# Sample states of branch A: four 32-row tiles on half-width spreads, one set of four banks

## What is computed

```python
def step(S, inp):
    r_t, w_t, k_t, v_t, kk_t, b_t = inp
    sk = jnp.einsum('bhvk,bhk->bhv', S, kk_t)
    S = S * w_t[:, :, None, :] - sk[..., None] * b_t[:, :, None, :] + v_t[..., None] * k_t[:, :, None, :]
    return S, jnp.einsum('bhvk,bhk->bhv', S, r_t)
S, ys = lax.scan(step, s_wkv.astype(f32), xs)
```

## Time and profile before

| what | value |
|---|---|
| median of three runs | 1308.31 us |
| lowest and highest run | 1305.56 us, 1309.54 us |
| the profiled execution's own time | 1308.13 us |
| its span, first to last instruction | 1306.4 us |
| PE busy | 1243.1 us (95%) |
| DVE busy | 862.6 us (66%) |
| ACT busy | 551.2 us (42%) |
| granted TensorE clock, mean | 0.984 |

### The profile page before, as it was taken

How to read it: one execution, slowest core, us unless ns; L and a number is a source line. 1 busy time by engine, 2 the same in 40 slices (tenths; PEclk the granted TensorE clock), 3 DMA queues, 4 the chain that set the end, 5 groups by cost and what they waited for, 6 DMA issues and landing times.

```text
span 1306.4 us, 27689 instructions
## 1 busy us (share of the span) xinstructions
PE 1243.1 (95%) x11984; PEld 1167.4 (89%) x11984; DVE 862.6 (66%) x1440; ACT 551.2 (42%) x841; POOL 128.4 (10%) x144
## 2 busy tenths in 40 slices
PE   6999999999998999999899998999999989999996
PEld 5899887898997999999798987888899979999996
DVE  4887568877766665653477954688777657566433
ACT  5553434443445433343444533344444454333432
POOL 0004473000000000000000071900000000000000
PEclk9999999999998999999999999999999989999998
DMA  6433235544353644544433323355444534444441
GB/s 225 129 116 115 66 104 177 196 146 146 127 168 101 189 146 149 157 146 147 144 97 113 125 75 86 95 181 181 145 147 134 160 101 145 147 154 146 151 149 69
DMA packets 51176, 179.50 MB, mean 137 GB/s; under 512 B 6256, under 2 KB 7024, under 8 KB 49776
## 3 DMA queue, kind: packets, MB, share of 16 engines
q1 hardware_dynamic: 42576, 153.77, 37.7%
q10 hardware_dynamic: 8480, 23.97, 5.2%
HBM read 166.57 MB, written 8.53 MB: 134 GB/s over the span
## 4 chain that ended last, share of the span: by engine, by line
PE 81%; DVE 8%; ACT 3%; POOL 3%; DMA 2%; issue 2%; ACTq 0%; SPq 0%; DVEq 0%; POOLq 0%
PE dense L1310 50%; PE core L1310 31%; DVE w_lo L857 2%; ACT w_hi L564 1%; DMA wkv_s<-s_st 1%; DVE x L905 1%; POOL qk_rot L521 1%; DVE y_out L903 1%; POOL rot_tmp L519 1%; POOL qk_rot L518 1%; DMA qk_rot<-qk_raw 1%; DMA x<-x_t 0%; POOL s_st L532 0%; DVE bonus L968 0%; DVE y_a L1164 0%
## 5 line engine op out<-in xcount | busy, mean ns | idle before, releaser
L857 DVE TENSOR_TENSOR w_lo<-w_raw,w_hi 128x1024 fp32r<-128x1024 f32 x282 | 350.9, 1245 | 237.3 <-ACT w_hi L564 236.8
L564 ACT ACTIVATE w_hi<-w_raw 128x1024 fp32r<-128x1024 f32 x282 | 298.0, 1057 | 474.8 <-PE dense L1310 317.3
L1310 PE MATMUL dense<-h_hi,w_hi 128*128 128x320 f32 x1296 | 418.4, 323 | 28.7 <-DVE h_lo L861 14.6
L1310 PE MATMUL dense<-h_hi,w_lo 128*128 128x320 f32 x1296 | 404.9, 312 | 0.0
L1310 PE MATMUL dense<-h_lo,w_hi 128*128 128x320 f32 x1296 | 404.8, 312 | 0.0
L1310 PEld LDWEIGHTS dense<-h_hi,w_hi 128*128 128x128 f32 x1296 | 247.0, 191 | 45.0 <-issue 33.5
L1310 PEld LDWEIGHTS dense<-h_lo,w_hi 128*128 128x128 f32 x1296 | 247.6, 191 | 4.3 <-issue 2.4
L1310 PEld LDWEIGHTS dense<-h_hi,w_lo 128*128 128x128 f32 x1296 | 247.3, 191 | 0.0
L1310 PE MATMUL core<-h_hi,w_hi 128*128 128x320 f32 x416 | 129.5, 311 | 0.0
L1310 PE MATMUL core<-h_lo,w_hi 128*128 128x320 f32 x416 | 129.0, 310 | 0.0
L1310 PE MATMUL core<-h_hi,w_lo 128*128 128x320 f32 x416 | 129.0, 310 | 0.0
(11 more groups left out here) (295 smaller groups left out, 1987.9 us busy)
## 6 DMA issues: line engine op xcount, KB each, us to landing
w_raw<-wts SPq DMA_DIRECT2D x282, 512.0 KB, 3.5
ret_t<-ret_t ACTq DMA_DIRECT2D x16, 256.0 KB, 3.7
ret_s<-ret_t ACTq DMA_DIRECT2D x16, 256.0 KB, 2.4
ret_rest<-ret_d ACTq DMA_DIRECT2D x2, 1536.0 KB, 6.6
qk_rot<-qk_raw SPq DMA_DIRECT2D x8, 320.0 KB, 6.2
dmask<-rconst ACTq DMA_DIRECT2D x2, 1152.0 KB, 5.6
s_st<-wkv_st ACTq DMA_DIRECT2D x2, 1024.0 KB, 5.0
wkv_s<-s_st ACTq DMA_DIRECT2D x2, 1024.0 KB, 8.1
```

The lines of the kernel that those rows point to most:

```text
L564: act.activation(w_hi[n % RING][:, :], w_raw[n % RING][:, :], ACT.Copy).then_inc(hi_ready.sem, 1)
L857: dve.tensor_tensor(w_lo[r][:, :], w_raw[r][:, :], w_hi[r][:, :].bitcast(F32), ALU.subtract).then_inc(low_made.sem, 1)
L1310: return pe.matmul(out, lhsT, rhs, start=start, stop=stop)
```

## The change

The spreads have 4 blocks instead of 8 (256 columns instead of 512): block s holds the tokens of sequence s of the first four and, in the other 32 rows of the half, those of sequence s + 4, since the pattern `F_SEQ` now repeats after four. So the rows 32q to 32q + 31 of a half (q = 0, 1) give the states of the sequences 4q to 4q + 3. A pair is eight matmuls of 32 rows by 64 output rows by 256 columns: the two heads, the two values of q, and v and u. All v results of q lie in `of_v[q]`, all u results in `of_u[q]`; these are four banks, half filled, and the same four for every pair. So a pair waits for the adds of the pair right before it, and the first pair for the add of the sample outputs (`y`), which lie in `core[3]`. DVE adds in four steps of 256 columns, three of them waited for. The spreads lie in other places (L200), which takes the wait for the transposed values out of the first one (L1051). `TAIL` has another order, and the first tile that opens `dense[2]` again waits for `s3` instead of `s2`.

```diff
-TAIL = [("gate", 0), ("s", 0), ("mean", 0), ("mean", 1), ("s", 1), ("gate", 1), ("mean", 2), ("mean", 3), ("s", 2), ("s", 3),
-        ("var", 0), ("var", 1), ("gate", 2), ("var", 2), ("var", 3)]
+TAIL = [("gate", 0), ("s", 0), ("mean", 0), ("mean", 1), ("s", 1), ("gate", 1), ("s", 2), ("mean", 2), ("mean", 3), ("gate", 2),
+        ("var", 0), ("var", 1), ("s", 3), ("var", 2), ("var", 3)]
...
-        v_exp, u_exp = [at("v_exp0", 20, 512), at("v_exp1", 22, 512)], [at("u_exp0", 32, 512), at("u_exp1", 34, 512)]
+        v_exp, u_exp = [at("v_exp0", 20, 256), at("v_exp1", 21, 256)], [at("u_exp0", 22, 256), at("u_exp1", 23, 256)]
...
-        def state_banks(h):
-
-            return (core[3], core[2]) if h % 2 else (dense[2], core[4])
+        of_u, of_v = (dense[2], core[3]), (core[4], core[2])
...
-                    return dve.tensor_tensor(to[h % 2][:, :].rearrange("p (s c) -> p s c", s=NSEQ), bc(of, 1, NSEQ),
-                                             bc(fx[:, F_SEQ:F_SEQ + NSEQ], 2, C), ALU.mult)
+                    return dve.tensor_tensor(to[h % 2][:, :].rearrange("p (s c) -> p s c", s=4), bc(of, 1, 4),
+                                             bc(fx[:, F_SEQ:F_SEQ + 4], 2, C), ALU.mult)
...
-                    if h == 0:
-                        dve.wait_ge(*v_turned(layer, 7))
...
-                        link(dve.tensor_tensor(st, st, state_banks(h)[0][:, :], ALU.add))
-                        dve.tensor_tensor(st, st, state_banks(h)[1][:, :], ALU.add).then_inc(seq_evac.sem, 1)
+                        for q in range(2):
+                            part = st[:, 256 * q:256 * q + 256]
+                            link(dve.tensor_tensor(part, part, of_v[q][:, 0:256], ALU.add))
+                            ins = dve.tensor_tensor(part, part, of_u[q][:, 0:256], ALU.add)
+                            if q == 0:
+                                link(ins)
+                        ins.then_inc(seq_evac.sem, 1)
...
-                        pe.wait_ge(*seq_evac(layer, EVAC_AT["s2", SAMPLE]))
+                        pe.wait_ge(*seq_evac(layer, EVAC_AT["s3", SAMPLE]))
...
-                        evac("ys", NCHUNK - 1)
-                    elif h == 1:
                         evac("y", SAMPLE)
                     else:
-                        evac(f"s{h - 2}", SAMPLE)
+                        evac(f"s{h - 1}", SAMPLE)
                     tk = step_mats(tok, SAMPLE, 128)[:, h, :]
-                    of_u, of_v = state_banks(h)
-                    across(of_v[:, :], tk[:, 0:C], v_exp[h % 2][:, :])
-                    done(halves(of_u[:, :], tk[:, C:2 * C], u_exp[h % 2][:, :]))
+                    for of, keys, spread, crossed in ((of_v, tk[:, 0:C], v_exp, 1), (of_u, tk[:, C:2 * C], u_exp, 0)):
+                        for q in range(2):
+                            for half in range(2):
+                                rows, to = slice(C * half + 32 * q, C * half + 32 * q + 32), C * (half ^ crossed)
+                                ins = mm(of[q][to:to + C, 0:256], keys[rows], spread[h % 2][rows, :])
+                    done(ins)
...
-    fixed[:, F_SEQ:F_SEQ + NSEQ] = (i // SEQ_S)[:, None] == np.arange(NSEQ)
+    fixed[:, F_SEQ:F_SEQ + NSEQ] = (i // SEQ_S % 4)[:, None] == np.arange(NSEQ)
```

More of the change, by code:

```diff
@@ L136 @@
 FILL = (2, 2, 1)
-ACT_STEPS, DVE_STEPS, POOL_STEPS = 13, 221, 18
+ACT_STEPS, DVE_STEPS, POOL_STEPS = 13, 229, 18
 def program(nc, x_t, wts, pvec, lora, shift0, fixed, rmask, trig, rconst, wkv_st, ret_d, ret_t,
```

## The result

The changed kernel takes 1300.82 us (median of nine runs, 1298.24 to 1303.85) against 1307.26 us before (nine runs, 1304.56 to 1309.57). The ratio is 0.9946, 95% interval 0.9930 to 0.9962: faster by 0.54%, 6 to 7 us (5.0 to 9.2 by the interval). The forecast was 1305.8 and its range began at 1303.6, so it was wrong: the gain is some three times as large. The profiled execution of the changed kernel is its fastest, 1298.24 us with a span of 1296.5.

What follows compares the result with a forecast made beforehand. PE was taken to set the pace inside the stage, with slack behind it, where time counts only through DVE's low part; 1308.1 + 0.3 (first layer) - 1.1 (second layer) - 1.5 (clock) = 1305.8 us, range 1303.6 to 1309.8.

Steps and rivals of the forecast that it cites:

- The products: PE's pair of matmuls in the stage: 0.62 us instead of 1.02, with eight 32-row tiles at work at once.
- two row tiles of one bank take turns: Rival at the pairs: four passes, 1.0 us a pair as now, total 1307.8 us; chance 0.08.
- The new wait: At pair 1 PE waits 1.7 us for DVE's adds of pair 0.
- the sum: Whole kernel: 1308.1 + 0.3 - 1.1 - 1.5 = 1305.8 us, the saving of all four pairs spent at pair 1.
- Pair 2: In the first layer PE waits 0.8 us for DVE's adds of pair 1, held behind a gain by ACT's lateness.
- "shorter wait" rival: Low part at 204.11 runs undisturbed, pair 1's wait 0.6 us shorter per layer: about 1304.5; 0.11 including luck with transfers.
- 0.55 us later: First head products behind the stage start 0.55 us late in each layer.
- The store and what follows: Second layer: store ahead of the weight load lands sooner than 9.28 us, so DVE's low part comes 1.1 us sooner.
- My 6.5: Landing time in us taken for the second layer's store of the states, between 5.0 and 9.3.
- my 2.3 for both layers: Forecast change over both layers: 0.3 us more in the first, 1.1 less in the second, 1.5 less for the clock.
- The clock at 898: Behind the second layer's second head products the fall at 898.6 stays away, saving 1.5 us.
- about 0.03 for four more starts: Term in the 0.62 us pair: about 0.03 us for PE's four added matmul starts.

Runs made afterwards that it cites:

- `pad64`: The kernel before with 16 inert fp32 matmuls (64 TensorE records) added ahead of the first pair of layer 1: 1302.31 us, ratio 0.9962.
- `before_again`: The kernel before, unchanged, measured once more: 1307.97 us, ratio 0.9993.
- `tiles_only`: The changed kernel with the old order of `TAIL` put back, keeping 32-row tiles and one set of four banks: 1312.62 us, ratio 1.0050 against the kernel before.
- `tail_only`: The kernel before with the new order of `TAIL` alone, 64-row tiles and two sets of banks kept: 1305.07 us, ratio 0.9987.
- `after_pad68`: The changed kernel with 17 more 8-column matmuls in layer 1, giving it 48 whole instruction blocks: 1301.85 us, ratio 0.9945 against the kernel before.
- `after_low1`: The changed kernel with DVE's four low parts in the rounds one round earlier in both layers: 1307.45 us, ratio 0.9993 against the kernel before.

## Why the prediction was wrong, step by step

- **The products**: right, 0.62 us. The rival that two row tiles of one bank take turns (1.0 us) is refuted here: `core` and `dense` banks each took two row tiles, on different halves of their rows, and all eight records of a pass started within 0.05 us, with the pair at 0.62 us. By the packing rate of the Trainium skill ("TensorE: Matmul & The Clock Gate", section "Part 3: Packing small matmuls — row/col tiling"), 3.07 for four 32-row tiles, the pair would have been an estimated 0.75 us; the trace has 0.62 us and shows no such loss. "No row of before has 32-row tiles" was not quite so: the trace has 16 records of 32 by 128 (`lora_w`, in layer 1 from 55.3 us on), but they start 0.37 us or more apart and say nothing of tiles at work together.
- **The new wait** at pair 1: 1.58 and 1.10 us for 1.7, right in size. It eats the gain of the tiles, as the sum said.
- **Pair 2**: wrong. I took ACT's lateness there for something "the change does not touch". In that execution ACT waited for POOL's rotations, which ended at 206.7; in the changed kernel's they ended at 203.8 and ACT's last wait was a store's landing, so its high part came at 204.93 instead of 207.26. That is no work of the change either: in `pad64`, with the wide spreads, the high part starts 0.4 us behind the first pair, in the profile of before 3.1 us, and in `before_again`, the same program, 1.6. I had taken one execution's lateness for the program's. It is the "shorter wait" rival, a fraction of a microsecond: without the 0.8 us of this wait the first head products come 19.9 and 19.5 us after the first pair (223.87, 864.71), as before (19.9, 19.4), and not 0.55 us later.
- **The store and what follows**: the mechanism held. Where a weight load is issued 0.1 to 1.1 us ahead of the store (the old order with 64-row tiles, four kernels, eight stores), the next transfer is issued 6.0 to 9.5 us after it; where it comes 1.2 us or more behind (the new order, nine kernels, eighteen stores), 4.1 to 6.1 us. `tiles_only` has the old order, but its load is issued 0.41 us behind the store, and there it is 4.9 us in both layers: this speaks for the load's place and not for the order as such. My 6.5 was too careful. From the first pair to the second head products the old order with 64-row tiles scatters from 44.5 to 47.3 us, the new order from 44.4 to 45.1 (leaving out layers with added products). No run moves that load alone, so this is read side by side, not taken apart. The order alone is worth 1.7 us by `tail_only` (from 3.9 us faster to 0.5 us slower by the interval), against my 2.3 for both layers.
- **The clock at 898**, the 1.5 us of it: not supported. `before_again` has the 2.18 us wait and no fall; the falls of 3.4 us come at other places in other executions (185, 796, 827 us). I had read cause and price from one example. In the rounds, falls do follow waits: all nine between 740 and 822 us in the fourteen traces start 0.5 to 1.7 us after PE went on from an issue wait of 1.75 us or more, but six waits of over 2 us have none behind them. A fall of 3.4 us at half the clock costs at most 1.7 us, so a part of what the moved block ends gave back may be clock.
- **The term that failed** is "about 0.03 for four more starts". I priced the added PE instructions by the time they take, and summed the stage alone since the rest was code "which the change does not touch". Their effect is on what stands behind them: 64 records in layer 1 move every block end of layer 2, and `pad64` puts that alone at 5.0 us (3.0 to 6.9). With the order's 1.7 this is 6.7, where the change measured 7.1. So the mechanism of the stage was sound but for pair 2 and the clock; what failed is that I took the code outside the stage to be out of its reach. The waits put to issue, 7.4 us between 740 and 822, were in the trace of before; I did not ask what set them.

The Trainium skill, "Runtime: NRT & Kernel Launch", section "Instruction fetch mechanics", says that instructions come in blocks of 16 KiB (256 instructions) by a DMA queue of the sequencer and that crossing into a new block is mostly hidden. The blocks agree with the trace: packets of 16 KB, and waits at a period of 256 records. That it is hidden does not hold in the rounds, where blocks follow each other every 3.5 to 4 us: one block cost PE 2.0 to 2.9 us where a weight load of 3.2 us stood ahead, and 1.48 us where none did.

What stays open: which of the waits a fall of the clock follows; why fewer waits (2.9 instead of 4.1 us) gave no time in `after_pad68`, whose profiled execution spends 9.9 us more at the lower clock than that of the changed kernel, the fastest of its nine; and how much of each execution's 5 us of spread comes from the same meetings of fetch and load.

## What to carry to other kernels

A kernel that is bound by one engine can have a cost that no stage shows: the place of its instruction-block ends against the large transfers. When a change adds or drops instructions on that engine, look for waits with no cause at a period of 256 instructions, and time a version that only pads the count before crediting the change with a small gain. Issue a transfer that somebody waits for ahead of bulk loads, not just behind one.

## What the runs showed of the hardware

- An instruction packet of 16 KB waits behind a weight load of 512 KB that is issued ahead of it: in the waits of over 2 us in layer 2 it started 2.9 to 3.4 us after the load's issue, and PE went on 2.2 to 2.8 us after the packet's start.
- With no load ahead, a packet started 1.4 to 1.5 us after PE reached the block before the one it carries, and PE could go on 2.4 to 2.6 us later: a block of 2.46 us of work then cost 1.48 us (four kernels).
- 16 products of 64 rows by 8 columns, computing nothing, made the kernel 0.38% faster (0.23 to 0.53%).
- A low part of 1.2 us on DVE took 6.02 us beside uninterrupted work of POOL (`after_low1`). The low part at the first pair took 1.88 to 1.90 us in the twelve layers of the fourteen traces in which POOL's last rotation ended after it had begun, and 1.21 or 1.22 us in the other sixteen.
